# Four selections moved to attention blocks 2, 3, 5 and 6, and the mixer's split and the first variance to block 7

## The reference

```python
out_a = gmlp_mixer(a_u, a_v, w_s, b_s, a_ln_g, a_ln_b)          # 256 columns
out_b = diff_attention(b_q, b_k, b_v, lam, lam_init, subln_g)   # 4 heads of 2 x 64, values of 128, then RMS norm
out_c = dsa_attention(c_q, c_k, c_v, i_q, i_k, i_w)             # 4 heads of 64 over the 256 best keys of each query
mix = jnp.concatenate([out_a, out_b, out_c], axis=-1)
x = layer_norm(DEEPNORM_ALPHA * x + jnp.einsum('bse,ed->bsd', mix, w_out), ln1_g, ln1_b)
```

## Time and profile before

| | us |
|---|---|
| median of 3 timed runs | 2201.16 |
| their range | 2199.04 to 2201.55 |
| the profiled execution | 2189.69 |
| its span, first to last instruction | 2187.9 |
| busy in the span: PE, DVE, ACT, POOL | 2108.8, 1100.7, 746.3, 178.4 |
| chain that ended last: PE, DVE, ACT | 82%, 9%, 6% |
| mean granted clock of TensorE | 0.98 of full speed |

### The profile page before, as it was taken

The page is one execution under the profiler, slowest core; times in us unless marked ns, Lnnn a source line. Parts: engine busy times, 40 slices in busy tenths (PEclk is TensorE's granted clock), DMA queues, the critical chain, the costliest instruction groups (busy, mean ns, idle before and its releaser), DMA issues.

```text
span 2187.9 us, 25880 instructions
## 1 busy us (share of the span) xinstructions
PE 2108.8 (96%) x9834; PEld 1694.3 (77%) x9834; DVE 1100.7 (50%) x1708; ACT 746.3 (34%) x1189; POOL 178.4 (8%) x159
## 2 busy tenths in 40 slices
PE   5999999999999999999988998999999999999998
PEld 4888888878888887588855667878788888888877
DVE  7743463664234373878888764483412222222146
ACT  3311124432112443655755654242111111111133
POOL 1000002300000231012210000310000000000000
PEclk6999999999999999999978999999999999999999
DMA  8433333222111422101110002221111111111131
GB/s 301 144 118 95 105 105 87 77 68 70 45 48 48 135 81 87 51 21 29 49 39 1 1 1 106 87 77 53 54 49 48 45 56 50 40 48 58 46 127 77
DMA packets 222092, 154.75 MB, mean 71 GB/s; under 512 B 6565, under 2 KB 209462, under 8 KB 221878
## 3 DMA queue, kind: packets, MB, share of 16 engines
q1 hardware_dynamic: 215392, 134.53, 20.1%
q0 software_dynamic: 4608, 16.78, 2.3%
q10 hardware_dynamic: 2006, 2.31, 0.3%
HBM read 145.21 MB, written 8.39 MB: 70 GB/s over the span
## 4 chain that ended last, share of the span: by engine, by line
PE 82%; DVE 9%; ACT 6%; issue 2%; DMA 1%; POOL 0%; ACTq 0%; DVEq 0%; POOLq 0%; SPq 0%
PE pair L2084 36%; PE pair L2101 17%; PE pair L2534 8%; PE pair L2287 4%; PE pair L2142 3%; PE pair L2421 3%; ACT proj L996 2%; PE pair L2389 2%; PE pair L2320 2%; PE pair L2604 1%; PE pair L2403 1%; PE pair L2308 1%; PE pair L2113 1%; DVE act_region L1698 1%; DVE w_lo L1321 1%
## 5 line engine op out<-in xcount | busy, mean ns | idle before, releaser
L1327 DVE TENSOR_TENSOR w_lo<-w_raw,w_hi 128x1024 fp32r<-128x1024 f32 x101 | 123.8, 1225 | 672.0 <-ACT w_hi L780 671.8
L780 ACT ACTIVATE w_hi<-w_raw 128x1024 fp32r<-128x1024 f32 x102 | 108.2, 1061 | 804.1 <-PE pair L2084 623.0
L2084 PE MATMUL pair<-act_hi,w_hi 128*128 128x512 f32 x1168 | 361.3, 390 | 1.8 <-ACT v_all L936 1.8
L2084 PE MATMUL pair<-act_lo,w_hi 128*128 128x512 f32 x1168 | 359.6, 389 | 0.0
L2084 PE MATMUL pair<-act_hi,w_lo 128*128 128x512 f32 x1168 | 359.6, 389 | 0.0
L2084 PEld LDWEIGHTS pair<-act_hi,w_hi 128*128 128x128 f32 x1168 | 218.9, 188 | 48.8 <-ACT v_all L936 2.2
L2084 PEld LDWEIGHTS pair<-act_hi,w_lo 128*128 128x128 f32 x1168 | 219.2, 188 | 45.7
L2084 PEld LDWEIGHTS pair<-act_lo,w_hi 128*128 128x128 f32 x1168 | 219.2, 188 | 45.6
L2101 PE MATMUL pair<-act_hi,w_hi 128*128 128x512 f32 x608 | 243.9, 401 | 4.2 <-DVE act_lo L1340 2.0
L2101 PE MATMUL pair<-act_lo,w_hi 128*128 128x512 f32 x608 | 237.7, 391 | 0.0
L2101 PE MATMUL pair<-act_hi,w_lo 128*128 128x512 f32 x608 | 237.6, 391 | 0.0
(11 more groups left out here) (407 smaller groups left out, 3157.5 us busy)
## 6 DMA issues: line engine op xcount, KB each, us to landing
w_raw<-w_in SPq DMA_DIRECT2D x76, 512.0 KB, 3.7
w_raw<-w_out SPq DMA_DIRECT2D x48, 512.0 KB, 3.8
w_raw<-w_gu SPq DMA_DIRECT2D x48, 512.0 KB, 3.7
w_raw<-w_down SPq DMA_DIRECT2D x24, 384.0 KB, 3.0
act_region<-w_ada SPq DMA_DIRECT2D x16, 512.0 KB, 13.4
sq<-w_ada POOLq DMA_DIRECT2D x16, 512.0 KB, 3.8
sq_sum<-w_ada POOLq DMA_DIRECT2D x16, 512.0 KB, 4.9
yT<-x SPq DMA_DIRECT2D x8, 512.0 KB, 7.4
```

The source lines that it names most:

```text
L780: A(w_hi[s_][:], w_raw[s_][:], ACT.Copy).then_inc(hi_ready, 1)
L1327: v.tensor_tensor(w_lo[s_][:], w_raw[s_][:], f32(w_hi[s_][:]), ALU.subtract)\
L2084: i = mm(bank[pair][:, h * HALF:(h + 1) * HALF], w[slot][:, k, :], a[:, k, h * HALF:(h + 1) * HALF], start=(k == 0 and w is w_hi and a is ...
```

## The change

- The selections of blocks 4, 5, 6 and 7 ran in the iterations of attention blocks 0, 1, 2 and 3. They now run in those of blocks 2, 3, 5 and 6 (SELECT_IN), one step for each item, as before.
- The ties (`same`) of these selections are written to `act_region[:, 0]` and no longer over the mixer's first column group.
- The mixer's split moves from the start of the loop to the first four items of block 7: ACT rounds chunk it in iteration 42 + it, behind its copy of the transposed map, and DVE subtracts it in the same iteration, where it waits for ACT.
- The variance of the first four blocks moves from iterations 25, 26 and 28 to 43, 44 and 46.
- POOL's low parts of units 14 and 15 wait until `c_out(6)` in iteration 42 is done; DVE takes note of POOL's sixteen low parts behind the loop.
- ACT rounds the weights of unit 15 behind its copy of unit 13, no longer ahead of it.

```diff
--- before.py
+++ after.py
@@ -72,6 +72,7 @@
 BITS_IN_UNIT = {2: 2, 3: 2, 4: 2, 5: 2, 6: 3, 7: 2, 8: 2, 9: 3, 10: 3}
 assert sum(BITS_IN_V) + sum(BITS_IN_UNIT.values()) == BITS
 EARLY_SEL = (SEL0, SEL0 + 1)
+SELECT_IN = {2: 4, 3: 5, 5: 6, 6: 7}
 
 
 def column(i):
@@ -706,7 +707,10 @@
             unit_lo(4)
             pool.wait_ge(dist_signed, 2)
             g.memset(dist_bias[0:CHUNK, T - CHUNK:T], MASKED).then_inc(dist_ready, 1)
-            for n in range(5, N_UNITS + 2):
+            for n in range(5, N_UNITS):
+                unit_lo(n)
+            pool.wait_ge(c_taken, TT - 1)
+            for n in range(N_UNITS, N_UNITS + 2):
                 unit_lo(n)
 
             def z_sum(a, ks):
@@ -1017,7 +1021,10 @@
             A(dist_bias[:], dist_bias[:], ACT.Copy, scale=-1.0).then_inc(dist_signed, 1)
 
             for n in range(2, N_UNITS):
-                unit_hi(n + 2)
+                if n < N_UNITS - 1:
+                    unit_hi(n + 2)
+                else:
+                    act.wait_ge(unit_done, 1 + U_PROJ + n + 2)
                 if n == MIX_AFTER - 2:
                     act.wait_ge(ln_var, 1)
                     A(ln_stat[:, 1], ln_stat[:, 1], ACT.Sqrt).then_inc(ln_rstd, 1)
@@ -1036,6 +1043,7 @@
                     A(proj[:, UNIT_SLOT[n], :], o, ACT.Copy).then_inc(p3_copied, 1)
                 for s_ in bits_in_unit(n):
                     bit_signs(s_)
+            unit_hi(N_UNITS + 1)
 
             def exps(item):
 
@@ -1056,10 +1064,6 @@
                 A(probT[g % 2][:, 0:n], bank[2][:, 0:n], ACT.Copy).then_inc(pT_copied, 1)
 
             exps(0)
-            for b in range(2):
-                for a in range(2):
-                    A(act_hi[:, b, a * HALF:(a + 1) * HALF], proj[:, S_AU + b, a * HALF:(a + 1) * HALF], ACT.Copy)\
-                        .then_inc(s_hi, 1)
             for k in range(N_ITEMS):
                 i, it = divmod(k, ITEMS)
                 if k + 1 < N_ITEMS:
@@ -1076,7 +1080,12 @@
                 if i and it == 2:
                     act.wait_ge(cT_done, i)
                     A(act_hi[:, 6:8, (i - 1) * P:i * P], cT_bank, ACT.Copy).then_inc(c_hi, 1)
-                if k == 4 * ITEMS + 2:
+                if i == TT - 1 and it < MIX_CHUNKS:
+                    b, a = divmod(it, 2)
+                    act.wait_ge(sel_done, N_TS)
+                    A(act_hi[:, b, a * HALF:(a + 1) * HALF], proj[:, S_AU + b, a * HALF:(a + 1) * HALF], ACT.Copy)\
+                        .then_inc(s_hi, 1)
+                if k == 7 * ITEMS + 2:
                     act.wait_ge(ob_var, 1)
                     A(o_ss[:, tiles(0)], o_ss[:, tiles(0)], ACT.Sqrt).then_inc(ob_rstd, 1)
             own.did(A(table[:], ones[:, 0:1], ACT.Sqrt))
@@ -1665,7 +1674,7 @@
 
                 q, n = column(i), keys(i)
                 t1, eq = thr_s[:, q:q + 1], buf_b[:, 0:n]
-                same = junk[:, 0:n] if i in EARLY_SEL else proj[:, S_AU, 0:n]
+                same = junk[:, 0:n] if i in EARLY_SEL else act_region[:, 0, 0:n]
                 if step == 0:
                     own.did(v.tensor_scalar(tile(i), tile(i), sign[:, q:q + 1], None, ALU.mult))
                 if step == 1:
@@ -1767,27 +1776,26 @@
                     biased(k + 1)
                 if it < BH:
                     combine(k)
-                if SEL0 + len(EARLY_SEL) + i < TT:
-                    select(SEL0 + len(EARLY_SEL) + i, it)
-                if k < MIX_CHUNKS:
-                    b, a = divmod(k, 2)
-                    dve.wait_ge(s_hi, SP_MIX + k + 1)
+                if i in SELECT_IN:
+                    select(SELECT_IN[i], it)
+                if i == TT - 1 and it < MIX_CHUNKS:
+                    b, a = divmod(it, 2)
+                    dve.wait_ge(s_hi, SP_MIX + it + 1)
                     v.tensor_tensor(act_lo[:, b, a * HALF:(a + 1) * HALF],
                                     proj[:, S_AU + b, a * HALF:(a + 1) * HALF],
                                     f32(act_hi[:, b, a * HALF:(a + 1) * HALF]), ALU.subtract).then_inc(s_lo, 1)
-                if k == MIX_CHUNKS:
-                    dve.wait_ge(pool_lo, N_UNITS + 2)
-                    dve.sem_inc(lo_ready, N_UNITS + 2)
                 if i and it == 0:
                     c_out(i - 1)
                 if i and it == 3:
                     c_low(i - 1)
                 if it == 5:
                     ob_squares(i)
-                if k == 4 * ITEMS + 1:
+                if k == 7 * ITEMS + 1:
                     ob_variance(0)
-                if k == 4 * ITEMS + 4:
+                if k == 7 * ITEMS + 4:
                     ob_scale(0)
+            dve.wait_ge(pool_lo, N_UNITS + 2)
+            dve.sem_inc(lo_ready, N_UNITS + 2)
             ob_variance(1)
             c_out(TT - 1)
             ob_scale(1)
```

## The result

| | before | after |
|---|---|---|
| median of 5 timed runs, us | 2200.84 (2199.04 to 2201.55) | 2212.79 (2210.77 to 2213.18) |
| ratio, with its 95% interval | | 1.0059 [1.0047, 1.0071] |
| the profiled execution, its span, us | 2189.69, 2187.9 | 2212.79, 2211.0 |
| mean granted clock | 0.980 | 0.974 |

The changed kernel is slower by 12 us. The forecast was 18.3 slower, 2219.5 in a range of 2204 to 2232.

What follows compares the result with a forecast made beforehand. PE (82% of the chain) bounds it, where it waits or runs at half clock. -1.9 - 2.9 - 5.2 - 3.2 - 1.5 + 3.0 + 16.5 + 13.5 = +18.3 us on median 2201.16: 2219.5, range 2204 to 2232.

Steps and rivals of the forecast that it cites:

- entry: Entry of the loop: POOL no longer holds DVE, so the first exponential waits only for ACT's table load; minus 1.9 us.
- block 4: Block 4 loses the variance chain, whose table loads held PE; minus 1.5 us, bounds minus 1.0 and minus 2.9.
- blocks 5 and 6: They gain 7.0 and 8.0 us of DVE selection work, partly hidden; plus 3.0 us for both, bounds 0 and plus 7.
- The large term: Block 7: DVE waits for ACT's rounding and PE for DVE's pass, making one chain; 13.1 + 3.4 = plus 16.5 us.
- Rival (4): Block 7's wait is hidden because PE doesn't wait for DVE's pass; -11.7, 2189.5 us; chance 0.07.
- The clock: Block 7: half clock behind each PE gap, 3 us for each of three, 4.5 for the last; plus 13.5 us.
- Rival (1): The clock holds in block 7, so no 13.5; +4.8, 2206 us; chance 0.12.
- rival (2): Early savings only 9, and the clock stays low right through block 7, costing 22; +32, 2233 us; chance 0.15.
- Rival (3): Blocks 0 and 1 run at full clock from item 2 on, 4 us more gained; 2215 us; chance 0.11.
- Blocks 0 to 3: Less selection and split work, clock recovering in block 1: block 0 minus 2.9, block 1 minus 5.2, blocks 2 and 3 minus 3.2.
- The early terms: The savings from the entry to block 4, 14.7 us, less what blocks 5 and 6 add: -11.7.
- The rule on POOL: Block 7: POOL holds item 43's combine on DVE until +8.8; 0.7 us at full clock, nothing at half, taken as 0.

Runs made afterwards that it cites:

- e1: The kernel before, unchanged, run again for a second profile: 2199.80 us, ratio 1.0007; its profiled execution took 2200.04 us.
- e6: The kernel after with unread products on PE in the four gaps of block 7, waits kept: 2204.50 us, ratio 1.0027.
- e2: The kernel after with ACT rounding each of the mixer's four chunks one item earlier (items 41 to 44): 2183.03 us, ratio 0.9946.
- e7: e2 with the selections of blocks 4 to 7 in blocks 3, 4, 5 and 6: 2184.60 us, ratio 0.9935.
- e12: e2 with unread products keeping PE busy at the entry of attention: 2183.12 us, ratio 0.9937.
- e9: The kernel before with the entry's three edits alone (POOL's wait, DVE's note of it, ACT's order): 2197.16 us, ratio 1.0002.
- e11: The kernel after with POOL's low parts of units 14 and 15 back at the entry: 2217.73 us, ratio 1.0092.
- e10: The kernel before with only the variance of the first four head outputs moved to block 7: 2197.03 us, ratio 0.9997.
- e3: The kernel after with the mixer's split back at the start of the loop: 2184.26 us, ratio 0.9950.
- e4: The kernel before with only the mixer's split (and the ties) moved as in the change: 2228.65 us, ratio 1.0141.
- e5: The kernel before with only the four selections moved to blocks 2, 3, 5 and 6: 2186.90 us, ratio 0.9944.
- e8: e7 with the rounding of unit 15's weights moved into block 5: 2183.59 us, ratio 0.9935.

## Why the prediction was right, and where its sum was off

| term | predicted | against the first profile | against e1's profile |
|---|---|---|---|
| ahead of attention (not the change) | 0 | +1.9 | +1.1 |
| entry | -1.9 | -1.9 | -1.9 |
| block 0 | -2.9 | -3.5 | -3.5 |
| block 1 | -5.2 | -6.3 | -2.5 |
| blocks 2 and 3 | -3.2 | -1.9 | -9.4 |
| block 4 | -1.5 | -1.9 | -1.9 |
| blocks 5 and 6 | +3.0 | +3.3 | +3.3 |
| items 42 to 44, wait and clock | +13.1 + 9 | +19.6 | +19.6 |
| item 45 to the copy of item 46 | +3.4 | +3.0 | +3.0 |
| from there to the end | +4.5 | +10.9 | +5.0 |
| sum | +18.3 | +23.1 | +12.8 |

(Both columns are cut at the transposes, as in the prediction.)

**The large term was right.** The chain of block 7 came as written: logits at +5.21 for +5.3 forecast, DVE waiting for ACT's rounding, PE for DVE's pass. At full clock the three items would be 30.6 us by the estimate from e6; the forecast was 30.7. e2 shows the cause by itself: the same work with the rounding one item ahead costs 3.3 us instead of 19.6 in the three items, and 1.6 instead of 3.0 behind them. These 1.6 are half clock behind the gap of 1.97 us; in e7 and e12, with the same gap, the clock held and they are 0. Rival (4), the hidden wait, fell with the 4.12 us ahead of PE's L2397.

**The clock** was forecast at 3 us for each of the three gaps and cost 6.6 together: the third stretch was only 3.5 us long. For the last gap 4.5 was set, and half clock cost 8.2 up to the heads' transposes (21.6 us for 13.4). This was the mis-sized term: it was priced as if the stretch ended within the 10 us of the last products, and it went on for 27.3 us. That the table's last column has +5.0 there, close to the 4.5, is luck: e1 has half-clock stretches of its own from 1343 on (6.9, 6.5 and 3.5 us), where after has the last 8 us of its long one and 4 us at 1492. Rival (1) fell with the clock of 0.77, and rival (2) too, for the clock came back between the gaps (stretches of 6.4, 7.4 and 3.5 us in 37.2). Rival (3) came half true: block 0 stayed at 0.50 and block 1 had 0.88, and the two took 27.6 us where the forecast has 29.3 and the rival 25.3.

**The entry** is exact, and e9 and e11 show it alone. **Blocks 5 and 6**, +3.3 for +3.0, and **block 4**, -1.9 for -1.5, came within their bounds; e10 gives block 4's -1.5 and a price of 0.5 in block 7 that the prediction put at nothing. In after the table loads do lie in the gap, and the wait of PE behind them, at item 45's values, is 1.11 us as in before; where the gap is closed it is 1.45 (e10, e3), and 1.97 with the rounding beside it (e2).

**Blocks 0 to 3** hold most of the distance from 12 to 18.3. The prediction read one execution and added its sum to a median of others, 11.5 us above, without asking what filled those 11.5 us. e1 answers: stretches of half clock in blocks 2 and 3 (53.1 us for 44.7), at the end of attention and at 1463 and 1480. Of the others with the selections in place, e4 and e10 have 56.3 and 52.9 us there, e9 46.3. In none of the kernels with the selections moved (after, e2, e3, e5, e6, e7, e8, e11, e12) do blocks 2 and 3 take over 43.3. So against an execution like e1's the change saves 9.4 us there, where the step had 3.2, and 2.5 in block 1, where it had 5.2 from a stretch of half clock that only the first profile and e9's have there. The early terms by medians are e3 against the 2198.6 us beside it, -14.4 (by the ratio, -11), for -11.7 forecast. The late split's 28.5 (24 by the ratios) stands for 16.5 + 13.5 = 30. The two make +14.1 against the 2198.6 us of before in that comparison, which is the measured 12.0 against the 2200.84 of the other. That 18.3 came as near as it did to 12 is in part luck: against the first profile the sum was 4.8 too small, by the end's clock and what lies ahead of attention, and against e1's 5.5 too large, by blocks 2 and 3.

Why DVE's larger selections go with these falls was not tried by itself. PE's waits behind the scan are the likely cause: with the selections in place PE idles 1.80 us in block 1, 1.42 to 1.87 in block 2, and 0.64 and 1.02 in block 3, and each fall between the entry's stretch and block 4 comes right behind one of them (before, e1, e4, e9, e10); with the selections moved 1.34 and 1.02 are the longest, and none falls. Which of the gaps brings the fall differs: the one in block 1 did in the first profile and in e9, and not in e1, e4 and e10.

**The rule on POOL.** The GPSIMD Engine Reference (Specifications) of the Trainium skill, by which POOL contends for its SBUF interfaces with DVE instructions that have two SBUF inputs, held: 1.88 and 1.86 us for 0.22 (e9, after), 2.92 for 0.75 (e11). The prediction had `combine` held until +8.8 behind item 42's transpose, and POOL let it go at +8.7. The forecast gave it 0.7 at full clock and nothing at half clock. At full clock PE waited 0.53 us (e9) and 0.52 (e2); at half clock e11 against after shows nothing.

## What to carry to other kernels

Work on an idle engine isn't free where an in-order partner has to wait for it: put the producer's part an iteration ahead of the consumer's, as e2 does, and the same move costs 3 us instead of 20. A gap of PE of about 4 us cost twice here, by its length and by half clock behind it: 3.5 to 7.4 us of it in the middle of block 7, and 27.3 us behind the last gap, where many small products follow (that these are the reason wasn't tested). And ahead of adding a difference to a median, ask what separates the profiled execution from that median.

## Unexpected of the hardware

- The clock falls at different places in executions of one program: between 1116 and 1500 us two profiles of the kernel before had 41 and 61 us at half clock, and took 2189.7 and 2200.0 us in all.
- The length of a short gap doesn't say whether the clock falls. The gap of 1.97 us at item 45 preceded about 3 us at half clock in e2 (1313.0 to 1316.3) and in e8; the same gap in e7 and e12 left it at 1.00. The one of 1.02 us at the end of block 3 stood right ahead of some 17 us at half clock in e1 (from 1196.8), e4 and e10, and of none in before and e9. Timeline of e7, PE:

```profile
1315.29 2.05 PE L2428 MATMUL pair<-v_all,act_region 128*128 128x128 f32 x16 [1.97 <-ACT act_region L1064]
```

- A DVE operation on one element for each partition, 0.22 us alone, was held 1.88 us until POOL's operation of 128x1024 was done (e9): what it is held for goes by the end of POOL's work, not by its own size. `combine`'s reciprocal (`den_r<-den`), with one operand, took its usual 0.16 us in after while POOL worked.
